# A hybrid encoder trunk on one core: routing in two sorted lists with a threshold, the first two experts gathered one at a time, and no meeting ahead of the RWKV pairs

## The reference, cut to what matters

```python
def expert_choice_ffn(h, w_router, w_gate, w_up, w_down):
    cap = EC_CAPACITY * s // N_EXPERTS                 # 64
    aff = jax.nn.softmax((h @ w_router).astype(jnp.float32), axis=-1)
    gates, idx = lax.top_k(jnp.swapaxes(aff, 1, 2), cap)
    xe = h[b_idx, idx]
    hid = silu(xe @ w_gate) * (xe @ w_up)              # per expert, 1024 x 1024
    ye = (hid @ w_down) * gates[..., None]
    return jnp.zeros_like(h).at[b_idx, idx].add(ye)

for i in range(DEPTH):
    x = x + mix_i(rms_norm(x, norm_mix_g[i]))
    x = x + expert_choice_ffn(rms_norm(x, norm_ffn_g[i]), ...)
```

## Time and profile before

| | |
|---|---|
| time, median of 3 runs | 1900.12 us (1898.45 to 1905.87) |
| profiled execution | 1901.98 us, its span 1900.2 us |
| mean granted PE clock | 0.977 of full |
| busy: PE, DVE, ACT, POOL | 1772.0, 819.0, 559.6, 153.1 us |
| start, pairs, layer 0 output and routing | 0 to 80, 80 to 592, 592 to 659 us |
| layer 0 experts, MLA, layer 1 output and routing | 659 to 1096, 1096 to 1363, 1363 to 1443 us |
| layer 1 experts | 1443 to 1900 us |

### The profile page before, as it was taken

How to read it: one execution, slowest core, us unless ns; L and a number is a source line. 1 busy time by engine, 2 the same in 40 slices (tenths; PEclk the granted TensorE clock), 3 DMA queues, 4 the chain that set the end, 5 groups by cost and what they waited for, 6 DMA issues and landing times.

```text
span 1900.2 us, 40296 instructions
## 1 busy us (share of the span) xinstructions
PE 1772.0 (93%) x17576; PEld 898.3 (47%) x17576; DVE 819.0 (43%) x1562; ACT 559.6 (29%) x1161; POOL 153.1 (8%) x230
## 2 busy tenths in 40 slices
PE   7999999999999599999988998999996999999998
PEld 4456666666555333333333355666543333333333
DVE  7867777776653412222211234777414222112212
ACT  3456555655542111111110123555320111101110
POOL 2101110111011100000000011111120000000000
PEclk9999999999999799999999998999997999999999
DMA  4101101110314999999999942000276999999998
GB/s 130 37 19 45 38 24 35 45 38 24 110 69 150 366 377 427 428 427 427 427 428 426 417 165 112 24 24 25 98 304 249 428 427 428 427 427 428 427 428 343
DMA packets 92184, 459.69 MB, mean 242 GB/s; under 512 B 16997, under 2 KB 50154, under 8 KB 68202
## 3 DMA queue, kind: packets, MB, share of 16 engines
q1 hardware_dynamic: 89994, 449.78, 58.5%
q0 software_dynamic: 2016, 7.34, 1.0%
HBM read 449.23 MB, written 7.86 MB: 241 GB/s over the span
## 4 chain that ended last, share of the span: by engine, by line
PE 73%; DMA 10%; issue 7%; DVE 3%; ACT 2%; SPq 2%; DVEq 1%; POOL 1%; POOLq 1%; another core or an unknown queue 1%; ACTq 0%; PEldq 0%
PE banks L1780 26%; PE banks L549 9%; DMA arena<-in_moe_w_down 7%; PE banks L1802 5%; PE banks L854 4%; PE banks L1433 4%; DMA arena<-in_moe_w_up 3%; PE banks L2355 3%; PE banks L2220 2%; PE banks L2380 1%; PE banks L2368 1%; PE banks L834 1%; PE banks L566 1%; SPq L1957 1%; PE banks L1748 1%
## 5 line engine op out<-in xcount | busy, mean ns | idle before, releaser
L1780 PE MATMUL banks<-arena 128*64 128x512 f32 x2944 | 657.4, 601 | 32.1 <-DMA arena<-in_moe_w_down 20.2
L1780 PEld LDWEIGHTS banks<-arena 128*64 128x64 f32 x2944 | 209.7, 138 | 442.7 <-issue 411.3
L1945 DVE TENSOR_TENSOR arena<-arena,banks 128x512 f32<-128x512 f32 x128 | 88.1, 688 | 285.1 <-PE banks L1802 285.1
L549 PE MATMUL banks<-arena 128*128 128x512 f32 x384 | 192.1, 618 | 0.0
L1885 ACT ACTIVATE arena<-banks 128x512 f32<-128x512 f32 x32 | 34.1, 1066 | 394.1 <-PE banks L1780 394.1
L1929 DVE SCALAR_TENSOR_TENSOR arena<-arena,banks 128x512 f32<-128x512 f32 x32 | 34.1, 1064 | 217.7 <-ACT arena L1885 217.7
L1802 PE MATMUL banks<-arena 128*128 128x512 f32 x256 | 114.7, 598 | 1.5 <-DVE arena L1942 1.5
L854 PEld LDWEIGHTS banks<-arena 64*64 64x64 f32 x5120 | 83.7, 134 | 62.9 <-issue 51.4
L1932 DVE SCALAR_TENSOR_TENSOR arena<-arena,small,banks 128x512 f32<-128x512 f32 x32 | 35.6, 1112 | 174.6 <-PE banks L1780 174.6
L854 PE MATMUL banks<-arena 64*64 64x64 f32 x5120 | 95.0, 221 | 2.6 <-issue 0.9
L549 PEld LDWEIGHTS banks<-arena 128*128 128x128 f32 x384 | 64.8, 189 | 51.5 <-issue 43.1
(11 more groups left out here) (307 smaller groups left out, 2217.7 us busy)
## 6 DMA issues: line engine op xcount, KB each, us to landing
arena<-in_moe_w_gate SPq DMA_DIRECT2D x64, 2048.0 KB, 32.5
arena<-in_moe_w_up SPq DMA_DIRECT2D x64, 2048.0 KB, 35.1
arena<-in_moe_w_down SPq DMA_DIRECT2D x54, 2048.0 KB, 36.2
arena<-in_moe_w_down SPq DMA_DIRECT2D x24, 512.0 KB, 11.6
arena<-in_moe_w_down SPq DMA_DIRECT2D x8, 1024.0 KB, 26.1
arena<-in_x SPq DMA_DIRECT2D x8, 512.0 KB, 7.5
arena<-in_rw_wr SPq DMA_DIRECT2D x8, 512.0 KB, 4.3
arena<-in_rw_wk SPq DMA_DIRECT2D x8, 512.0 KB, 4.2
```

Of the source, the lines that this page charges most:

```text
L549: last = nc.tensor.matmul(b[:, :], w_sl[:, n, k, :], xmix[n][:, k, :], start=(k == 0), stop=(k == ND - 1))
L1780: last = nc.tensor.matmul(b[z * CAP:(z + 1) * CAP, :], st[:, k, :], ring[g % RING][:, k, z * 512:(z + 1) * 512], start=(c % 2 == 0 and k = ...
L1945: nc.vector.tensor_tensor(xs, xs, b[:, :], ALU.add).then_inc(free[xj[("add", i, j)][0]], 1)
```

## The change

Three edits. (1) Start: the masks and four of the five level masks are built on DVE ahead of the first normalised tile; the meeting ahead of the pairs is gone (counts go on from the start into the pairs), so PE can form the first LR block after the first half of the operands, and some last work of the start (`gate_quarters_pe`, `gates_dve`) stands inside the first pair. SP loads pair 1's weights as slots are read. (2) Routing: tiles 0 to 2 are routed as an "early" list (16 x 384) while the output product of tile 3 still runs, tile 3 as a "late" list (16 x 128). Eight rounds go over each; the threshold is the least of the elementwise maxima of one list and the other reversed. It is sent to all partitions by two transposes, and a token's rank comes from eight small products with a triangle (`upto`) and ones (`every`). (3) The first pair's tokens are gathered for one expert at a time, each half with 64 columns of `pick`.

```diff
 def route_dve(dve, layer):
-    (mask, tensor_tensor_scan, product, transposes back)
+    merged = late_work[0:NE, 0:CAP]
+    nc.vector.tensor_tensor(merged, early_top[0:NE, :], late_top[0:NE, ::-1], ALU.max)
+    nc.vector.tensor_reduce(limit[0:NE, 0:1], merged, AX, ALU.min)
+    nc.vector.tensor_scalar(early_work[0:NE, 0:CAP], merged, limit[0:NE, 0:1], None, ALU.is_gt)
+    nc.vector.tensor_reduce(limit[0:NE, 1:2], early_work[0:NE, 0:CAP], AX, ALU.add)
+    nc.vector.tensor_copy(wide_limit[0:NE, :, :], ...).then_inc(limit_ready, 1)
...
 out_pe:
+    for i in range(2):
+        nc.tensor.matmul(rank[:, i, :, :], upto, above[:, i, :, :], start=(i == 0), stop=False, skip_group_check=True)
+        for t in range(NT - 1):
+            nc.tensor.matmul(rank[:, i, t + 1:NT, :], every, above[:, i, t:t + 1, :].to_broadcast([P, later, NE]), ...)
...
 out_dve, after turned(2):
+    largest(0, NT - 1, "sel_early")
+    shares(0, NT - 1, "sel_early")
+    added(3, 0)
+    listed("at_early", early_work)
+    for r in range(3):
+        early_round(r)
+    added(3, 1)
+    early_round(3)
+    turned(3)
+    early_round(4)
+    largest(3, NT, "sel_late")
+    dve.sem_inc(hT_read[n], 1)
+    shares(3, NT, "sel_late")
+    early_round(5)
+    listed("at_late", late_work)
+    (8 rounds on the late list, 2 on the early one beside them)
...
-def gather_half_pe(pe, z, xj):
+def gather_half_pe(pe, z, e, xj):
     for t in range(NT):
         for k in range(4):
-            nc.tensor.matmul(b[:, k * P:(k + 1) * P], h_tok[:, t, ...], pick[:, t, :], ...)
+            nc.tensor.matmul(b[:, k * CAP:(k + 1) * CAP], h_tok[:, t, ...], pick[:, t, e * CAP:(e + 1) * CAP], ...)
...
 moe_pe, pair 0, after gate of expert 0:
+    for z in range(2):
+        gather_half_pe(pe, z, 1, xj)
+    rows_pe(pe, 0, layer)
+    combination_pe(pe, 0, xj)
...
 every engine:
-    meet(pe, "pe")      # ahead of pairs_pe
 pairs_pe:
+    pe.wait_ge(operands_ready, 2 * u + 1)
     across(pe, "LR", Bt[0], 0, u)
+    if not u:
+        gate_quarters_pe(pe)
+        values_turned()
+    pe.wait_ge(operands_ready, 2 * u + 2)
     across(pe, "LR", Bt[1], 1, u)
```

More of the change, by code:

```diff
@@ L525, in trunk @@
             order += [(("g", u), 6), (("y", 0, u), 0), (("y", 1, u), 1)]
[L526 to L533, removed]
+        rj = Jobs(order + [(("yT", NPAIR), 6)], pj.count)
+        nth = lambda jb, u: u + (2 if jb is rj else 1)
         def bc(v, *shape):
@@ L762, in start_dve, with normed @@
         def start_dve(dve):
-            dve.wait_ge(ld_gain[0], 16)
-            for t in range(NT):
+            def normed(t):
+                if t == 0:
+                    dve.wait_ge(ld_gain[0], 16)
                 dve.wait_ge(rstd_ready, t + 1)
@@ L780, in start_dve @@
             turned(2)
[L781 removed]
+            level_dve(dve, 4)
             turned(3)
@@ L1415, in trunk @@
             order += turns(t)
-        ojs = [Jobs(order + routing, rj.count)]
+        ojs = [Jobs(order + routing(2, 3), rj.count)]
         order = []
@@ L1420, in trunk @@
         FIRST_OUT_BANK = 7
-        ojs += [Jobs([(name, FIRST_OUT_BANK if name == ("out", 0, 0) else bank) for name, bank in order + routing])]
+        NORMED = (NT, 0)
+        ojs += [Jobs([(name, FIRST_OUT_BANK if name == ("out", 0, 0) else bank) for name, bank in order + routing(0, 1)])]
         ojs[0].at[("out", *HELD)] = rj[("part", *HELD)]
@@ L1480, in out_pe @@
                 turn_x(1)
-                out(3, 0)
+                out(3, 0, range(3))
                 logits(1)
                 turn_x(2)
-                out(3, 1)
-                logits(2)
             else:
@@ L1489, in out_pe @@
                 pe.wait_ge(router_ready, 1)
-                for t in range(1, NT):
+                for t in range(1, NT - 1):
                     out(t, 0)
@@ L1528, in logits, with exponentials @@
                 nc.scalar.copy(lgT[:, tile(t)], b[:, 0:P]).then_inc(free[6 + t % 2], 1)
+            def exponentials(name, ts, count):
+                b = job_full(act, oj, name)
+                act.wait_ge(logit_ready, count)
+                for t in ts:
+                    last = nc.scalar.activation(logit[:, t, :], b[:, t * NE:(t + 1) * NE], ACT.Exp, bias=rmax[:, t:t + 1], scale=rstd4[:, t:t + 1],
+                                                accum_out=rsum_t[:, t:t + 1])
+                last.then_inc(free[oj[name][0]], 1)
             if n == 0:
@@ L1539, in out_act @@
                 scaled(1)
-                turned(2)
-                logits(2)
-                square(3)
             else:
                 square(0)
-                for t in range(1, NT):
+                for t in range(1, NT - 1):
                     turned(t - 1)
@@ L1617, in out_dve @@
                 turned(1)
-                added(3, 0)
-                turned(2)
-                added(3, 1)
             else:
-                for t in range(1, NT):
+                for t in range(1, NT - 1):
                     added(t, 0)
@@ L1699, in trunk @@
             order += [(("rows", i), 2)]
-            order += [(("x", i, 0), 0), (("x", i, 1), 1), (("comb", i), 2)]
+            order += [(("x", i, 0), 0), (("x", i, 1), 1)] if i else [(("x", 0, z, e), z) for e in range(2) for z in range(2)]
+            order += [(("comb", i), 2)]
             for e in range(2):
```

323 lines of the change are left out of this document (203 added, 120 removed).

## The result

The changed kernel takes 1918.25 us (median of five runs), against 1900.7 for the kernel before (median of five). Four of the five lie from 1914.03 to 1918.97 us; the fifth took 2331.85 us at a mean granted clock of 0.743 and is left out of the ratio. The ratio is 1.0078, 95% interval 1.0064 to 1.0092, which is 14.8 us slower. The forecast was 1905.6, 5.5 us slower, with a range to 1912: the direction was right, but the cost is nearly three times the forecast one, and every run lies above the range.

A forecast was written before the change was run, and what follows sets the result against it. The prediction took the start of gapless weight transfers to set the end of each expert stage. Start -8.7, gathers +13.2 and later first gathers +1.0 made +5.5 on the 1900.12 median: 1905.6 us, range 1888 to 1912.

The forecast's parts named there:

- Start: From kernel start to the first inverse step: 3.3 us from the first mix and 5.4 behind the operands, 8.7 gained (5.5 to 10).
- the start gives nothing lasting: First pair stays bound by ACT's copies or POOL, losing 3 to 8 of the 8.7 us: 1909 to 1914; 12 in 100.
- What bounds the kernel: Expert stages: the end is fixed by when weight transfers start running without a gap, 20.7 us after the first half gather before.
- The hole ahead of chunk 13: First experts of each layer: transfers idle 6 to 8 us before chunk 13; its bytes start 6.6 us later a layer.
- covered: PE's delay ahead of chunk 13 falls where transfers still have work, leaving only start and G: 1892.5; 8 in 100.
- the gather goes by its columns: A 64-column half gather takes 1.9 us, so the gapless stretch begins 7.7 us earlier, twice: about 1888; 12 in 100.
- From the end of the first gather to chunk 13: First pair's experts: SP issues chunk 13 some 25.6 us after the first half gather ends, with chunk 0 at full speed.
- The first half gather: Start of each layer's experts: 4.5 us instead of 5.88, because the rank products keep PE busy just ahead.
- Routing: Routing ahead of the experts: split lists win 2.8 us, closing takes 7.2 for 3.5; `picks` 1.5 late a layer (-1 to +4).
- the last tile waits: Tile 3's add 3.6 us late, plus clock fall and POOL's lock: `picks` 4 us late a layer, 1910.6; 14 in 100.
- The sum: Whole kernel: -8.7 for the start, +13.2 for the gathers, +1.0 for G in two layers, +5.5 in all.
- G: The moment a layer's first half gather ends; forecast 0.1 to 1 us late, 0.5 on average.

## Why the prediction was wrong

- **Start: right.** -8.7 forecast, -7.9 in the trace, -10 by the runs of the start alone. The first output product of layer 0 stands between 589.6 and 591.8 us in the three traces with the old start and between 579.9 and 583.9 in the eleven with the new one, on average 8.8 us sooner; one pair of traces is uncertain by 2 us here. The first mix came at 23.17 (23.5 forecast), the inverse step at 84.85 (84). The rival "the start gives nothing lasting" fell.
- **What bounds the kernel: right.** The end follows the moment from which the transfers have no gap. By the issue at 1484.49 and the forecast's 1.7 us behind it, chunk 13's bytes began at 1486.2 in layer 1, 16.8 us later than before (the first of them stand in the stretch from 1485.0 to 1485.5), and the span ended 17.0 later. The other traces say the same: from the end of chunk 13's issue to the end of the span it is 432.5 to 432.9 us in the four kernels that gather in two parts ahead of chunk 2, and 433.3 to 433.9 in the eight in which chunk 13 goes right behind chunk 12; in the last two the hole stands ahead of chunk 15, whose issue ends 422.1 and 422.7 us before the end, two chunks of 4.9 us less. The hole ahead of chunk 13 is in the windows, with almost no bytes from about 1478 to 1485, and 6 to 8 us were forecast; the rival "covered" fell, and so did "the gather goes by its columns": 3.79 us at a granted clock of 1.00 for 64 columns, 3.84 forecast.
- **From the end of the first gather to chunk 13: right but for chunk 0.** 25.6 us forecast, 27.0 measured in layer 1 and 27.8 in layer 0. Chunk 0 was taken at 3.65 and took 5.22 and 5.96; the rest agrees within 0.2 us.
- **The first half gather: the step that failed most.** I put it at 4.5 us, with the reason that "the rank products keep PE busy just ahead of the first half gather". It took 7.09 in both layers, 2.6 more. My price of a 64-column product came from rows with 3, 16 and 128 columns at the full clock, and the rise of the clock from a gather with 128 columns. With chunk 0, which I put at the full clock too, this is 4.2 us in layer 1 and 4.9 in layer 0. Three runs show what held: without rank products the gather is 7.09 too, and with nothing changed but the columns, 128 for 64, it is 5.4 to 5.9 and chunk 0 is 3.65. Over all traces the first gather took 7.09 in each of the six layers with 64 columns and 5.17 to 6.72 in each of the 22 with 128.
- **Routing: direction right, size a little small.** `picks` was put 1.5 us late and is 2.1. The add of tile 3 and the rank products (3.6 us, 3.8 forecast) are where I put them. The rival "the last tile waits" had the mechanism, since moving the early list won the 2 us back in the trace, but at 2 us and not 4. The fall of the clock in that wait, which I had as a condition for 2.5 us, came in part: the logits of tile 3 took 1.08 us for 0.65 in both layers, its transposes 1.97 for 1.09 in layer 1 alone.
- **The sum.** 2 x 0.6 for `picks` and 9.1 for gather and chunk 0 are 10.3; the start gave 0.8 less; layer 0's first gather before was 5.17 and not the 5.88 of layer 1, which I had counted twice, 0.7. With -0.8 for the assumption that G moves by 0.5 a layer, where its terms were 1.5 - 1.4 = 0.1, that is 11.0 of the 11.5 by which the span passed the forecast. This is the account of the traced execution, the longest of the four; two others took 1914.03 and 1914.98 us at a mean granted clock of 0.978 for 0.974, and by the ratio the change costs 14.8 us and not 17.0.

By the Trainium skill ("TensorE: Matmul & The Clock Gate", "Back-to-back issue gap") a product of 1 to 64 columns has a gap of about 60 cycles against 134 for 128. No run here shows that for float32 with a stationary block loaded for each product: 0.115 us an instruction with 64 columns (7.36/64) and 0.116 with 128 (7.41/64). The measurement decides.

What stays open: what it is in a 64-column stream that leaves the granted clock at the lower level (columns were changed, nothing else was separated from them), and why the clock fell behind the same 64-column gathers of the second expert in some layers and runs and not in others (16.54 and 15.65 us for the same chunks, against 13.96). That 128 columns keep it from falling there is seen in one run (13.95 in both layers) and not shown, since the changed kernel with 64 columns has 13.95 and 13.96 too. A late place for the second gathers without the new wait was not tried, since the hidden rows lie over the tokens that are gathered.

## What to carry to other kernels

Splitting a product by its moving columns saved nothing here, where each instruction loads its own float32 stationary block (7.36 us for 64 instructions with 64 columns, 7.41 with 128): count the instructions, and price them at the clock that this stretch will have, which a row with other columns does not tell. Where a queue of transfers sets the end, each chunk behind the hole has only the difference between transfer and compute as room for moved work (1.3 us here); more than that moves the hole and doesn't close it. Work that is moved takes its readers with it on the other engines, so look at what is queued behind them (here DVE's copy of the transposed `pick`, which held a bank twice) before it is called free.

## What the runs showed of the hardware

- 32 float32 instructions with 64 columns streamed for 7.09 us at a granted clock of 0.50 from first to last, in both layers, with the rank products ahead and without them (six layers of three kernels). With 128 columns, all else equal, the clock rose to 1.00 within the gather (0.50, 0.66, 1.00 in successive stretches of 2 us) and it took 5.40.
- Work made shorter just ahead of a stretch at the lower clock gave part of it back: with the first gather of layer 1 2.0 and 3.1 us sooner, it took 6.39 and 6.72 us for 5.36, and in layer 0 6.58 and 6.67 for 6.20. First gathers with 128 columns vary from 5.17 to 6.58 us between kernels without these edits as well, so how much of it the edits did is not shown.
- The rank products in bfloat16 took 0.4 us for 3.6, with half the instructions; the granted clock was 0.50 in both.
